# Sample values in side-by-side high and low tokens, column-grouped state reads, and GLA decays computed one head ahead, in a two-layer recurrent trunk

## The reference

```
# branch A, mLSTM, 4 heads, key size 128, value size 256; state C (256x128) and n (128)
w   = (q k^T) * exp(D - m_t)                    # inside a chunk
num = w v + s_inter * (C q)                     # C: state before the chunk
den = sum_s w + s_inter * (n q)
h   = num / max(|den|, exp(-m_t))
C_new = decay*C + (v wk)^T k ;  n_new = decay*n + sum_s wk k

# branch B, GLA, 4 heads, key size 128, value size 256; state S (128x256)
log_a = log_sigmoid(glr @ w_gla_lr2 + b_gla_gate) / 16
b     = cumsum(log_a)
o     = A v + (q exp(b)) S ,   A_ts = sum_d q_td k_sd exp(b_td - b_sd)
S_new = exp(b_L) S + (k exp(b_L - b))^T v
```

## Time and profile before

| | µs |
|---|---|
| median of 3 runs | 3322.17 (3321.14 to 3323.59) |
| the profiled execution: its own time | 3323.95 |
| its span | 3322.2 |
| PE busy | 3208.6 (97%) |
| DVE busy | 1930.4 (58%) |
| ACT busy | 1010.7 (30%) |
| chain of waits, by engine | PE 73%, DVE 15%, ACT 6%, issue 3%, DMA 1% |

### The profile page before, as it was taken

How to read it: one execution, slowest core, us unless ns; L and a number is a source line. 1 busy time by engine, 2 the same in 40 slices (tenths; PEclk the granted TensorE clock), 3 DMA queues, 4 the chain that set the end, 5 groups by cost and what they waited for, 6 DMA issues and landing times.

```text
span 3322.2 us, 58852 instructions
## 1 busy us (share of the span) xinstructions
PE 3208.6 (97%) x24852; PEld 3161.6 (95%) x24852; DVE 1930.4 (58%) x2653; ACT 1010.7 (30%) x961; POOL 7.4 (0%) x24
## 2 busy tenths in 40 slices
PE   7999999999999999999999999999999999999997
PEld 7999989989999989999999999899999999899997
DVE  5434466667777875424454345666777788654344
ACT  3222222322333643212232123222222346432122
POOL 0000000000000000000000000000000000000000
PEclk9999999999999999999999999999999999999999
DMA  3222222322222212222222222232222222222221
GB/s 141 79 103 79 87 99 89 125 90 78 78 77 85 81 68 89 79 98 84 81 89 85 98 79 98 80 131 89 91 78 77 77 86 82 78 89 73 102 76 67
DMA packets 51745, 292.21 MB, mean 88 GB/s; under 512 B 9224, under 2 KB 12040, under 8 KB 23736
## 3 DMA queue, kind: packets, MB, share of 16 engines
q1 hardware_dynamic: 37440, 243.60, 21.5%
q10 hardware_dynamic: 13696, 46.32, 3.8%
q0 software_dynamic: 512, 0.94, 0.1%
HBM read 269.33 MB, written 21.50 MB: 88 GB/s over the span
## 4 chain that ended last, share of the span: by engine, by line
PE 73%; DVE 15%; ACT 6%; issue 3%; DMA 1%; DVEq 0%; ACTq 0%; SPq 0%
PE stream_b L384 32%; PE stream_a L384 31%; PE stream_a L458 5%; ACT wh L736 2%; DVE wl L1020 2%; PE stream_b L458 1%; DVE hsq L1233 1%; DVE xc L1453 1%; PE mix L488 1%; DVE tg L1011 1%; DVE tg L1305 1%; DVE Cst L1209 1%; DVE wS L1389 1%; ACT L931 1%; DMA out_o_ss<-CS 1%
## 5 line engine op out<-in xcount | busy, mean ns | idle before, releaser
L736 ACT ACTIVATE wh<-stage 128x2048 fp32r<-128x2048 f32 (+2 forms) x246 | 436.0, 1772 | 834.1 <-PE stream_b L384 590.2
L1020 DVE TENSOR_TENSOR wl<-stage,wh 128x2048 fp32r<-128x2048 f32 (+2 forms) x248 | 525.7, 2120 | 146.9 <-ACT wh L736 129.3
L384 PE MATMUL stream_a<-xh,wh 128*128 128x272 f32 x2560 | 544.8, 295 | 26.6 <-DVE wl L1020 16.3
L384 PE MATMUL stream_b<-xh,wh 128*128 128x272 f32 x2560 | 538.2, 292 | 9.2 <-DVE lyg L1011 6.9
L384 PE MATMUL stream_a<-xh,wl 128*128 128x272 f32 x2560 | 535.7, 291 | 0.0
L384 PE MATMUL stream_a<-xl,wh 128*128 128x272 f32 x2560 | 534.7, 291 | 0.0
L384 PE MATMUL stream_b<-xh,wl 128*128 128x272 f32 x2560 | 530.0, 288 | 0.0
L384 PE MATMUL stream_b<-xl,wh 128*128 128x272 f32 x2560 | 529.6, 288 | 0.0
L384 PEld LDWEIGHTS stream_a<-xh,wh 128*128 128x128 f32 x2560 | 409.8, 192 | 35.0 <-issue 24.1
L384 PEld LDWEIGHTS stream_b<-xh,wh 128*128 128x128 f32 x2560 | 403.5, 189 | 13.9 <-DVE lyg L1011 7.8
L384 PEld LDWEIGHTS stream_a<-xh,wl 128*128 128x128 f32 x2560 | 409.9, 192 | 0.0
(11 more groups left out here) (324 smaller groups left out, 4668.8 us busy)
## 6 DMA issues: line engine op xcount, KB each, us to landing
stage<-in_w_up SPq DMA_DIRECT2D x88, 1024.0 KB, 4.8
stage<-in_w_mix SPq DMA_DIRECT2D x88, 1024.0 KB, 4.8
stage<-in_w_down SPq DMA_DIRECT2D x32, 768.0 KB, 4.2
stage<-in_w_down SPq DMA_DIRECT2D x32, 640.0 KB, 3.8
CS<-in_c ACTq DMA_DIRECT2D x8, 1024.0 KB, 4.7
out_o_sc<-CS ACTq DMA_DIRECT2D x8, 1024.0 KB
CS<-in_s ACTq DMA_DIRECT2D x8, 1024.0 KB, 4.8
out_o_ss<-CS ACTq DMA_DIRECT2D x8, 1024.0 KB
```

The costliest lines, as they stand in the source:

```text
L384: mm = [pe.matmul(out(h), a(h), b(h), start=f, stop=z) for h in range(2)]
L736: act.activation(wh[:, slot, 0:width], stage[:, slot, 0:width], ACT.Copy).then_inc(hi_done, 1)
L1020: tt_(wl[:, slot, 0:width], stage[:, slot, 0:width], wh[:, slot, 0:width].bitcast(F32), ALU.subtract).then_inc(split_done, 1)
```

## The change

Four things change.

1. **Sample values.** POOL copies the 32 sample tokens of `xh` and of `xl` side by side into a new buffer `xs` (64 columns for each contraction step). The stationary side of the sample value group is then both at once, and two passes (by `wh` and by `wl`) take the place of three: 16 matmuls instead of 24. The products of the high tokens come out in one group of 32 output rows, those of the low tokens in the next; DVE adds the two with one more operation (`tmpv`).
2. **State reads.** `state_reads` puts the 32 sample queries on the stationary side (32 columns) and streams the 256 columns of each of the eight states, into four groups of 32 output rows: 8 matmuls of 256 columns. Each gives all 32 tokens for one state, of which 4 are wanted. ACT copies the bank to SBUF (`hsq`), and two matmuls for each half with the 0/1 matrix `pick` select and transpose. This replaces 16 matmuls of 4 columns.
3. **One column of n.** The 128 columns behind the values become one; where all 128 were needed as a stationary side, a broadcast of the one column or `ones` is used.
4. **GLA decays one head ahead.** The decay matmuls of head i+1 run in the outputs of head i, in banks 2 and 3; DVE takes z there, ACT forms the logarithm behind the square of head i, and DVE scans behind the sample states. The first GLA head of a layer stays as it was. The wait for `root_done` moves to the scores.

In the mLSTM head the column sum for the mean also moves: from between the last two gate tiles to behind two contraction steps of the second. In the GLA head the chunk outputs of the first value half run ahead of the state reads. PE's GLA loop now has its first and last head apart, and ACT's four GLA heads are written out.

```diff
@@ POOL
+            pool.memset(pick[:], 0.0)
+            pool.memset(xs[:].bitcast(F32), 0.0)
...
+            for L in range(DEPTH):
+                pool.wait_ge(acc_ready, L * (3 * KT) + 2 * KT)
+                for e, src in enumerate((xh, xl)):
+                    ins = pool.tensor_copy(xs[:, 0:KT, e * NS:(e + 1) * NS], src[:, :, T:N].bitcast(F32))
+                ins.then_inc(xs_ready, 1)
@@ PE, value_tiles
+                both = xs.rearrange("p k t -> p (k t)")
+                for k in range(KT):
+                    for b, f, z in ((wh, k == 0, False), (wl, False, k == KT - 1)):
+                        mm = pe.matmul(pair[1][:, 0, 0:DV], both[:, k * 2 * NS:k * 2 * NS + P],
+                                       b[:, j, k * DV:(k + 1) * DV], start=f, stop=z)
@@ PE, state reads
-            def sample_states(b_, v, out_col, lhs_of):
+            def state_reads(b_, done):
                 for s_ in range(SEQS):
...
+                    g, h = s_ % 4, s_ // 4
+                    mm = pe.matmul(Q[g * NS:(g + 1) * NS, b_, h * DV:(h + 1) * DV], qs[:, T:N], CS[:, s_, :],
+                                   start=True, stop=True)
+                mm.then_inc(done, 1)
+            def sample_states(b_, v, out_col):
+                for h in range(2):
+                    c0_ = h * DV + v * P
+                    mm = pe.matmul(Q[:, b_, out_col:out_col + NS], hsq[:, 0, c0_:c0_ + P], pick[:, h, :],
+                                   start=False, stop=h == 1, skip_group_check=True)
@@ PE, mlstm_head
-                        pe.matmul(Q[:, c, 0:DV + P], Kw[:, c, :], val[:, c, :], start=True, stop=True).then_inc(a_u, 1)
+                        pe.matmul(Q[:, c, 0:DV + 1], Kw[:, c, :], val[:, c, :], start=True, stop=True).then_inc(a_u, 1)
...
+                pair_block(n + 2, t + 4, 0, updates, ((), ((KT - 2, reads),)))
...
                 over_chunks(2)
+                pe.wait_ge(a_rows_read, B + 1)
+                sample_out(0)
...
-                pair_block(n + 3, t + 6, 1, mean, ((), ((2, lambda: sample_updates(1, 3, a_us)), (6, third))))
+                pair_block(n + 3, t + 6, 1, None, ((), ((2, mean), (7, third))))
@@ PE, gla_head, outputs
                     pe.wait_ge(b_c, B * NC + NC)
+                    if not last:
+                        decays(B + 1, 2)
+                    chunk_outputs(0)
                     pe.wait_ge(b_cs, B * 16 + 16)
+                    if not last:
+                        pe.wait_ge(b_zin, B + 2)
+                    state_reads(3, b_rd)
+                    chunk_outputs(1).then_inc(b_out, 1)
+                    pe.wait_ge(b_rows_read, B + 1)
@@ ACT, gla_head
+                act.wait_ge(b_rd, B + 1)
+                act.activation(hsq[:, 0, 0:2 * DV], Q[:, 3, :], ACT.Copy).then_inc(b_rows_read, 1)
                 next(gates)
                 act.wait_ge(b_h, B + 1)
                 act.activation(hsq[:], Hh[:], ACT.Square).then_inc(b_sq, 1)
+                if i + 1 < HEADS:
+                    log_decays(L, i + 1)
                 next(gates, None)
@@ DVE, take_sample_values
+                link(ts_(tmpv[:], src[NS:2 * NS], rstdT[NS:2 * NS, NC:NC + 1], None, ALU.mult))
+                stt(val[0:NS, NC, 0:DV], src[0:NS], rstdT[0:NS, NC:NC + 1], tmpv[:],
+                    ALU.mult, ALU.add).then_inc(tile_free, 1)
@@ DVE, gla_head
                     states(c, DV, lambda c_: eb[:, c_ * C + C - 1:(c_ + 1) * C], lambda c_: c_, b_u, b_c, B * NC)
+                if not last:
+                    take_decays(L, i + 1, 2)
                 masked_keys(Kf[0:NS]).then_inc(b_keys, 1)
...
+                    if not last:
+                        sum_decays(L, i + 1)
```

More of the change, by code:

```diff
@@ L588, in mlstm_head, with decays, gla_head @@
                 sample_updates(3, 3, a_us)
-            def gla_head(L, i):
+            def decays(B, b_):
+                pe.wait_ge(b_lr, B * 16 + 16)
+                for h in range(2):
+                    mm = pe.matmul(Q[:, b_ + h, 0:HALF], lr2[64:80, :], xg[64:80, h * HALF:(h + 1) * HALF],
+                                   start=True, stop=True)
+                mm.then_inc(b_z, 1)
+            def gla_head(L, i, first=False, last=False):
                 B = L * HEADS + i
@@ L593, in gla_head @@
                 t = L * LAYER_TILES + i * HEAD_TILES + (TILE_MIX + GATE_TILES + HEADS * HEAD_TILES)
-                pe.wait_ge(b_lr, B * 16 + 16)
-                pe.wait_ge(root_done, L * (2 * HEADS) + HEADS + 1 + i)
-                for h in range(2):
-                    mm = pe.matmul(Q[:, h, 0:HALF], lr2[64:80, :], xg[64:80, h * HALF:(h + 1) * HALF],
-                                   start=True, stop=True)
-                mm.then_inc(b_z, 1)
+                if first:
+                    pe.wait_ge(root_done, L * (2 * HEADS) + HEADS + 1 + i)
+                    decays(B, 0)
                 pair_block(n, t, 0)
@@ L696, in _ @@
                     mlstm_head(L, i)
-                with pe.Fori(0, HEADS) as i:
+                gla_head(L, 0, first=True)
+                with pe.Fori(1, HEADS - 1) as i:
                     gla_head(L, i)
+                gla_head(L, HEADS - 1, last=True)
                 with pe.Fori(0, KT // 4) as i:
@@ L858, in mlstm_head @@
                 next(gates)
[L859 removed]
                 act.wait_ge(a_c, B * NC + NC)
                 act.dma_start(o_pc[L, i], Cst[:, NC - 1, 0:DV + 1]).then_inc(state_stored, 16)
+                act.wait_ge(a_rd, B + 1)
+                act.activation(hsq[:, 0, 0:2 * DV], Q[:, 3, :], ACT.Copy).then_inc(a_rows_read, 1)
+                next(gates)
+                split_hi(nh + 2, 0, t + 5, 2 * D)
                 next(gates)
@@ L963, in mix @@
                 mlstm_head(L, HEADS - 1, last=True)
-                with act.Fori(0, HEADS - 1) as i:
+                for i in range(HEADS):
                     gla_head(L, i)
-                gla_head(L, HEADS - 1, last=True)
                 act.wait_ge(heads_done, L + 1)
@@ L1532, in mix @@
                 chain.hold()
-                with dve.Fori(1, HEADS) as i:
+                with dve.Fori(1, HEADS - 1) as i:
                     gla_head(L, i)
+                chain.hold()
+                gla_head(L, HEADS - 1, last=True)
                 chain.restart()
```

150 lines of the change are left out of this document (90 added, 60 removed).

## The result

| | before | after |
|---|---|---|
| median of 4 runs, µs | 3322.39 (3321.14 to 3323.59) | 3291.49 (3286.38 to 3292.03) |
| ratio | | 0.9904, 95% interval 0.9886 to 0.9921 |
| span of the profiled execution | 3322.2 | 3289.3 |
| PE in flight | 3208.6 (97%) | 3146.4 (96%) |

The kernel became 1% faster: 31 µs by the medians, where I forecast 35 (3287, range 3257 to 3310). That the sum comes so close is in part luck: the term for the mLSTM heads is 9 µs too large, and of the 7 µs that offset it 2 lie in the GLA boundaries and 5 in stretches to which I gave no gain. So the parts are worth a look.

A forecast was written before the change was run, and what follows sets the result against it. Each stage was read from the engine ending it: a PE-DVE loop in mLSTM heads, a chain through the sample-state store at changed GLA boundaries. 3324.0 - 24 - 11 = 3289, 3287 against the runs' median; range 3257 to 3310.

The forecast's parts named there:

- the term for the mLSTM heads: Eight mLSTM heads: three edits on the loop of PE and DVE gain 24 µs in all.
- Sample values, -0.95 a head in mLSTM: PE between sum and next scores: 16 matmuls for 24, 1.90 µs for 2.85, so -0.95 a head.
- One column of n, -0.53: DVE's state operations in an mLSTM head: 257 columns instead of 384 save 0.53 µs.
- The column sum behind two steps, -1.5: Last gate tile of an mLSTM head: 1.5 µs of PE work moves ahead of the mean's wait, so -1.5 a head.
- the -3.0 of the sum: mLSTM head: sample values, one column of n and moved column sum together shorten each head by 3.0 µs.
- The clock "costs nothing, since PE is not last there": GLA, PE's wait for the square sum: the clock may fall there, at no cost.
- The GLA loop, 78.8 for 80.7: GLA boundary: a chain through the sample-state store (8.4 µs) ends last, 78.8 µs for 80.7; each gains 1.9.
- PE waits about 3.5 µs for the square sum: GLA heads: PE waits about 3.5 µs before the sample update after the square sum, where it waited at most 0.9.
- Reads, 2.0 between 0.9 and 3.8: State reads on PE, per head: 0.9 µs if column groups run side by side, 3.8 if serial; 2.0 taken.
- The slower rival, 3364: State reads: column groups do not pipeline, reads take 9.1 µs a head, kernel slows to 3364 µs; chance 0.05.
- their term: Six boundaries between GLA heads: 1.9 µs gained at each, 11 µs in all.
- No new wait, 3257: GLA boundaries: the store does not hold up the high part, boundary 73.8 µs, kernel 3257 µs; chance 0.15.

The follow-up runs named there:

- experiment 6: Changed kernel with the sample values again from 24 matmuls (three passes) and one DVE operation: 3290.85 µs, ratio 0.9908.
- experiment 3: Changed kernel with the mLSTM mean's column sum and first sample updates back ahead of the last gate tile: ratio 0.9956.
- experiments 2, 4 and 10: Changed kernel, in this order, with: 12 unused matmuls filling the mean's wait, 0.9890; column sum behind four steps, 0.9889; full-width state reads, sample outputs uncomputed, 0.9894.
- experiment 11: Changed kernel with 28 unused matmuls in PE's wait for the square sum of each GLA head, load still directly behind the store: 3292.58 µs, ratio 0.9910.
- experiment 1: Changed kernel with ACT's store wait and load of the next sample states moved behind the next high part and four exponentials: 3274.45 µs, ratio 0.9856.
- experiment 9: Changed kernel with each of a head's eight state reads issued eight times in a row: 3559.60 µs, ratio 1.072.
- experiment 8: Changed kernel with late state load, mean behind four steps and 28 unused matmuls in each GLA head's square-sum wait: 3261.64 µs, ratio 0.9818.

## Why the prediction was right, and where it was not

- *Sample values, -0.95 a head in mLSTM.* Right between k and scores: -1.0 in the trace, and +1.0 in the middle heads when undone; over whole layers experiment 6 doesn't show it. That it gives nothing in a GLA head with the store on the loop was right as well.
- *One column of n, -0.53.* Right: -0.53 between scores and sum. It was not undone on the chip.
- *The column sum behind two steps, -1.5.* The step that failed: nothing came of it where the clock fell. The 12 matmuls did move ahead of the wait, and undoing it costs 17 µs (experiment 3). But I took a µs of PE work behind the wait for a µs at full clock. The wait grew to 2.0 µs because the reads in front of it had become cheaper, the granted clock fell behind it in five heads, and 3.4 µs at the low level cost 1.7. Without the fall the head is 65.9 (experiments 2, 4 and 10), which is the -3.0 of the sum. The four heads with a new fall gain 1.1 to 1.5 each and not 3.0, which is 6.7 of the 9.3 µs that the mLSTM term fell short. The rest lies in the first heads of the layers, which have no wait for the mean and gain 2.1 and 2.4, and in the last ones (2.6 and 2.3). In the first layer's first head the fall behind the values' wait is a likely part of it; no experiment takes it away.
- *The clock "costs nothing, since PE is not last there".* I wrote this for GLA and it held while the store was on the loop (experiment 11). For mLSTM I never asked the question: the earlier trace rows had shown a harmless fall, and I did not look where the next one would land.
- *The GLA loop, 78.8 for 80.7.* Right in its mechanism and nearly in every piece: decays and z, the 14.1 to the output copy, ACT's 9.5, the store's 8.5 for 8.4, 16.3 to the scores. The mean is 78.2. The edit to ACT's order took it off (experiment 1). My base of 80.7 was the first layer's; over both it was 80.4.
- *PE waits about 3.5 µs for the square sum.* It waits 5.0 in the middle heads. The reads were 1.07 and not 2.0, which accounts for 0.9 of the 1.5.
- *Reads, 2.0 between 0.9 and 3.8.* At the lower end. In one column group, back to back, a pass is 0.172 µs, so sixteen would be 2.8.
- *The slower rival, 3364.* Excluded as to its premise by the rows of L517. By experiment 9 its sign was right, and its price some 10 to 25 µs too high.
- *The closeness of the total.* The stretches outside the two branches gave 4.3 µs that no term of mine has, and the boundaries 2.0 more than their term; without these the kernel would have come out near 3298, still in the range.
- *No new wait, 3257.* It was not this kernel, but it is close to what comes when the store is moved away and the clock kept up: 74.8 a boundary in experiment 8 against its 73.8, 3262 against 3257.

## What to carry to other kernels

When an edit makes an engine faster ahead of a wait, the wait grows, and a longer wait on TensorE can lower the clock of what stands behind it: price work that follows a wait at both clock levels, and check which engine is last there. Work moved ahead of the wait, or even work thrown away, can then shorten the kernel, but only where TensorE is last behind the wait; the same filling gave 9 µs in one version and nothing in another. And when a calculation is moved out of a place, look at what it had covered there: here the logarithm had hidden the landing of a store, and moving the load behind the next work of the queue was worth half as much as the whole change.

## What the hardware showed

- Passes of 32 stationary columns to four column groups in turn cost 0.067 µs each, in one group back to back 0.172, and full-width passes with 256 columns to stream 0.226. The factor of 3.4 between the last and the first is for four groups. The Trainium skill ("TensorE: Matmul & The Clock Gate", Part 3: Packing small matmuls) gives 2.38 for three, and the trace agrees in kind. Its bullet there, that a weight load overlaps matmuls in flight only where the row group differs, doesn't hold for these reads: all have the same rows and differ in their columns alone, and sixteen passes with a weight load of 0.11 each, 1.75 µs of loads, end after 1.07. (The same part also lets a load run ahead into a background weight buffer; that would fit, and no run here tells which of the two it is.) The value tiles' passes of the same 256 columns cost 0.119. Those read rounded operands, the reads do not; which difference between them makes the factor of 1.9 was not tried.
- Of the six waits for the mean in the changed kernel, 2.0 to 2.5 µs long, five had a fall of the clock behind them and one had not, at the same place of the program. In experiment 6 it was four of six (2.0 to 2.2 µs), in the kernel before one of three (1.75 to 1.86), and in experiments 2 and 4 none of six each (0.5 to 1.0).
- The store of 1 MB took 8.4 to 8.7 µs in the changed kernel and up to 9.6 in experiment 11.
